# Hybrid SSD and sparse-attention layer: a new order of the weight units, and later SSD and norm steps

## What is computed

```
h = rmsnorm(x) * (1 + scale) + shift                      # scale, shift, gate from c @ w_ada
z, xbc, dt, q, kv, gates, za, mg = split(h @ w_in)
xs, B, C = split(silu(causal_conv4(xbc)))                 # 2048, 4*128, 4*128 channels
y = ssd(xs, softplus(dt), B, C) + d_skip * xs             # 2 chunks of 128, 32 heads, 4 groups
y_ssm = (rmsnorm_per_group(y * silu(z)) * g) @ w_ssm_out
kc, vc = silu(blocks(kv) @ w1) @ w2                       # 15 compressed blocks of 32 tokens
o = g0 * attend(q, kc, vc) + g1 * attend(q, ks, vs) + g2 * attend(q, kw, vw)
y_nsa = (o * silu(za)) @ w_nsa_out
out = x + gate * rmsnorm((sig(mg0) * y_ssm + sig(mg1) * y_nsa) @ w_out)
```

## Time and profile before

| | us |
|---|---|
| median of 3 runs (472.07 to 472.74) | 472.73 |
| profiled execution | 470.02 |
| its span, first to last instruction | 468.2 |
| PE busy | 438.0 |
| DVE busy | 356.2 |
| ACT busy | 259.1 |
| POOL busy | 233.9 |

### The profile page before, as it was taken

One profiled execution on the slowest core, in us unless ns is written; L12 is line 12 of the kernel. 1 busy time (PEld: TensorE's weight loads), 2 busy tenths in 40 slices (PEclk: granted clock), 3 DMA queues, 4 the chain that ended last, 5 costly groups with the idle time before them and its releaser, 6 DMA issues.

```text
span 468.2 us, 9862 instructions
## 1 busy us (share of the span) xinstructions
PE 438.0 (94%) x3636; PEld 399.7 (85%) x3636; DVE 356.2 (76%) x617; ACT 259.1 (55%) x512; POOL 233.9 (50%) x236
## 2 busy tenths in 40 slices
PE   2689989999999989999899988999999999999995
PEld 2387989999999989987898987988998989999874
DVE  0466789999999999678799986688797767547733
ACT  3235885655564653456786936566475555534441
POOL 0154662368788689755363532245355362445440
PEclk9979999999999999999999999999999999999998
DMA  7999544564424444436449550735646444456102
GB/s 280 417 415 372 182 134 136 187 191 143 158 90 146 170 137 135 136 136 241 160 183 357 162 160 0 270 98 189 256 161 243 139 136 139 165 190 228 47 0 90
DMA packets 22391, 84.04 MB, mean 179 GB/s; under 512 B 2492, under 2 KB 2882, under 8 KB 21186
## 3 DMA queue, kind: packets, MB, share of 16 engines
q1 hardware_dynamic: 22344, 83.42, 50.5%
HBM read 82.36 MB, written 1.05 MB: 178 GB/s over the span
## 4 chain that ended last, share of the span: by engine, by line
PE 69%; DVE 8%; issue 7%; ACT 5%; POOL 4%; DMA 4%; SPq 1%; DVEq 0%; POOLq 0%; ACTq 0%
PE gemm L703 14%; PE gemm L705 14%; PE gemm L704 14%; DMA w_ada_shift_scale<-in_w_ada 3%; PE y_or_o L910 2%; DVE w_lo L1191 2%; PE gemm L679 2%; ACT w_hi L932 2%; PE y_or_o L791 1%; ACT probs L1149 1%; DVE conv_acc L1238 1%; POOL w_lo L1534 1%; PE score L874 1%; PE gemm L662 1%; PE small L584 1%
## 5 line engine op out<-in xcount | busy, mean ns | idle before, releaser
L1534 POOL TENSOR_TENSOR w_lo<-w_raw,w_hi 128x256 fp32r<-128x256 f32 (+1 forms) x117 | 135.4, 1162 | 178.9 <-ACT w_hi L932 144.2
L703 PE MATMUL gemm<-h_hi,w_hi 128*128 128x256 f32 x600 | 172.3, 287 | 4.5 <-DVE conv_acc L1238 2.0
L705 PE MATMUL gemm<-h_hi,w_lo 128*128 128x256 f32 x600 | 167.2, 279 | 0.0
L704 PE MATMUL gemm<-h_lo,w_hi 128*128 128x256 f32 x600 | 167.2, 279 | 0.0
L1191 DVE TENSOR_TENSOR w_lo<-w_raw,w_hi 128x768 fp32r<-128x768 f32 (+1 forms) x117 | 130.8, 1118 | 38.7 <-ACT w_hi L932 38.2
L932 ACT CAST w_hi<-w_raw 128x1024 fp32r<-128x1024 f32 x117 | 122.3, 1045 | 49.4 <-PE gemm L705 29.3
L703 PEld LDWEIGHTS gemm<-h_hi,w_hi 128*128 128x128 f32 x600 | 113.3, 189 | 8.3 <-issue 2.8
L704 PEld LDWEIGHTS gemm<-h_lo,w_hi 128*128 128x128 f32 x600 | 113.0, 188 | 0.7 <-issue 0.2
L705 PEld LDWEIGHTS gemm<-h_hi,w_lo 128*128 128x128 f32 x600 | 113.1, 188 | 0.0
L703 PE MATMUL gemm<-ynorm_hi,w_hi 128*128 128x256 f32 x128 | 36.4, 284 | 0.0
L705 PE MATMUL gemm<-ynorm_hi,w_lo 128*128 128x256 f32 x128 | 35.6, 278 | 0.0
(11 more groups left out here) (252 smaller groups left out, 895.0 us busy)
## 6 DMA issues: line engine op xcount, KB each, us to landing
w_raw<-in_wpack SPq DMA_DIRECT2D x133, 512.0 KB, 4.4
w_ada_shift_scale<-in_w_ada SPq DMA_DIRECT2D x8, 1024.0 KB, 15.8
x_T<-in_xT SPq DMA_DIRECT2D x2, 512.0 KB, 6.2
x_residual<-in_x_tok SPq DMA_DIRECT2D x1, 1024.0 KB, 4.8
out_tok_dram<-out_tok SPq DMA_DIRECT2D x4, 256.0 KB, 2.1
ada_gate_products<-in_gate_bias SPq DMA_DIRECT2D x1, 512.0 KB, 4.5
g_post_rows<-in_g_post_rows SPq DMA_DIRECT2D x1, 512.0 KB, 5.6
consts<-in_consts SPq DMA_DIRECT2D x1, 272.0 KB, 22.1
```

Source lines behind the costliest of these rows:

```text
L703: nc.tensor.matmul(bank[:, 0:SEQ], w_hi, hi[:, k0 + k, :], start=first, stop=False)
L704: nc.tensor.matmul(bank[:, 0:SEQ], w_hi, lo[:, k0 + k, :], start=False, stop=False)
L705: last = nc.tensor.matmul(bank[:, 0:SEQ], w_lo, hi[:, k0 + k, :], start=False, stop=end)
L1534: nc.gpsimd.tensor_tensor(WL[:, n % LO_SLOTS, c:1024], RAW[:, u % RAW_SLOTS, c:1024], WH[:, n % HI_SLOTS, c:1024], ALU.subtract).then_inc( ...
```

## The change

From unit 10 on, the conv tiles c1 to c3 and x0 to x15 alternate with z0 to z15 and za0 to za4; the last of these stand alone. Units 0 to 9 and from 50 on are as before. The number of units and instructions is the same, and every unit's work is the same.

The cb steps go from units 15–17 to 18–20. The SSD groups start at b = 25 + 8g, five units later, and in the last group all from y6 on one unit later still: y6 at 54, y7 at 58, ysq3 at 59, ysum3 at 61 (before: 48, 52, 53, 55). blk0 and blk1 move by five units for the first three groups and the last stands at 43 and 44. ssq1 goes from unit 58 to 64. Norm tiles 0 to 7 stay where they are at their first step (units 51 to 61); tile 8 starts at unit 66 instead of 62, and the rest follows to unit 75. kcp goes from unit 61 to 63, and W2 is loaded after unit 63 instead of unit 60. The squares' sums get a place of their own, so POOL's clearing of k_lo no longer waits for ssq1.

```diff
--- before.py
+++ after.py
@@ -1,3 +1,5 @@
+import itertools
+
 import numpy as np
 
 import concourse.bass as bass
@@ -40,10 +42,10 @@
 def weight_units():
 
     units = [("pair", i, half) for half in range(2) for i in range(len(PAIRS))]
-    units += [("c", j, 0) for j in range(1, 4)]
-    for g in range(SSM_GROUPS):
-        units += [("x", TPG * g + j, 0) for j in range(TPG)] + [("z", TPG * g + j, 0) for j in range(TPG)]
-    units += [("za", j, 0) for j in range(5)]
+    convs = [("c", j, 0) for j in range(1, 4)] + [("x", j, 0) for j in range(TPG * SSM_GROUPS)]
+    gates = [("z", j, 0) for j in range(TPG * SSM_GROUPS)] + [("za", j, 0) for j in range(5)]
+    for conv, gate in itertools.zip_longest(convs, gates):
+        units += [conv, gate] if conv else [gate]
     for n, part in enumerate((0, 2)):
         units += [("w1k", 0, part), ("w1k", 0, part + 1), ("za", 5 + n, 0)]
     for split, part in ((("za", 7, 0), 0), (None, 2)):
@@ -100,26 +102,27 @@
     put(10, ("dtC", 0))
     put(13, ("acs", 0))
     for kind in range(3):
-        put(15 + kind, ("cb", kind))
+        put(18 + kind, ("cb", kind))
     for g in range(SSM_GROUPS):
-        b = 20 + 8 * g
+        b = 25 + 8 * g
+        last = g == SSM_GROUPS - 1
         put(b, ("xt", (g, 0)))
         put(b + 1, ("xt", (g, 1)), ("seg", 2 * g))
         put(b + 2, ("ea", 2 * g))
-        put(b + 4, ("y", 2 * g), ("seg", 2 * g + 1))
-        put(b + 5, ("ea", 2 * g + 1))
-        last = g == SSM_GROUPS - 1
-        put(b + 7 + last, ("y", 2 * g + 1))
-        put(b + 8 + last, ("ysq", g))
-        put(b + 10 + last, ("ysum", g))
+        put(b + 4 + last, ("y", 2 * g), ("seg", 2 * g + 1))
+        put(b + 5 + last, ("ea", 2 * g + 1))
+        put(b + 7 + 2 * last, ("y", 2 * g + 1))
+        put(b + 8 + 2 * last, ("ysq", g))
+        put(b + 10 + 2 * last, ("ysum", g))
     for g in range(KV_GROUPS):
-        put(18 + 8 * g, ("blk0", g))
-        put(19 + 8 * g, ("blk1", g))
+        put(min(23 + 8 * g, 43), ("blk0", g))
+        put(min(24 + 8 * g, 44), ("blk1", g))
     put(47, ("clear", 0))
     put(48, ("ssq", 0))
-    put(58, ("ssq", 1))
+    put(64, ("ssq", 1))
     tiles = TPG * SSM_GROUPS
-    norm_units = [u for u in range(50, len(UNITS)) if UNITS[u][0] not in NATIVE or UNITS[u][2] % 2]
+    norm_units = [u for u in range(50, 62) if UNITS[u][0] not in NATIVE or UNITS[u][2] % 2]
+    norm_units = norm_units[:tiles // 2] + list(range(66, len(UNITS)))
     for j in range(tiles + 2):
         for ahead, name in ((2, "ynlo"), (1, "ynhi"), (0, "yn")):
             if 0 <= j - ahead < tiles:
@@ -127,7 +130,7 @@
     at = UNITS.index
     put(at(("w1k", 0, 3)) + 2, ("hidT", 0))
     put(at(("w1v", 0, 3)) + 2, ("hidT", 1))
-    put(at(("w1v", 0, 3)) + 1, ("kcp", 0))
+    put(at(("w1v", 0, 3)) + 3, ("kcp", 0))
     put(at(("w1v", 0, 3)) + 4, ("vcp", 0))
     put(at(("vs", 1, 0)) + 2, ("vt", 0))
     put(at(("w1v", 0, 3)) + 3, ("zero", 0))
@@ -314,7 +317,7 @@
     V = place("v", [P, 2, 2, KV_GROUPS, HEAD_DIM], f32)
     over_at = cursor[0]
     kb = 1024
-    assert over_at + 50 * kb <= 229344, over_at
+    assert over_at + 52 * kb <= 229344, over_at
 
     ADA = place("w_ada_shift_scale", [P, 2, KT, 1024], f32, at=z_at)
     XT = place("x_T", [P, KT, SEQ], f32, at=over_at)
@@ -336,7 +339,7 @@
     CE = place("cb_decay_across", [P, 4, P], f32, at=over_at + 14 * kb)
     SQ = place("y_sq", [P, 4, SEQ], f32, at=over_at + 16 * kb)
     YT = place("y_tmp", [P, 2, SEQ], f32, at=over_at + 20 * kb)
-    SQS = place("y_sq_sums", [P, SSM_GROUPS, SEQ], f32, at=q_at + 28 * kb)
+    SQS = [place(f"y_sq_sums{n}", [P, 2, SEQ], f32, at=over_at + (22, 50)[n] * kb) for n in range(2)]
     RN = place("rstd_y", [P, SSM_GROUPS, SEQ], f32, at=q_at + 32 * kb)
     BLK = place("cmp_blocks", [P, 2, 16, KV_GROUPS * N_CMP], f32, at=over_at + 24 * kb)
     KVC = place("kv_cmp_T", [P, 4, SEQ], f32, at=over_at + 32 * kb)
@@ -538,7 +541,7 @@
                     else:
                         sp.wait_ge(native_mm, NATIVE_IDX[v] + 1)
                 sp.dma_start(RAW[:, u % RAW_SLOTS, :], wpack[u]).then_inc(w_in[u % RAW_SLOTS], 16)
-                if u == UNITS.index(("w1v", 0, 0)) + 4:
+                if u == UNITS.index(("w1v", 0, 0)) + 7:
                     wait_y_full(sp, ("y", 7))
                     sp.dma_start(W2[:], w2_dram).then_inc(w2_in, 16)
                 if u == UNITS.index(("kw",1,0)):
@@ -798,7 +801,7 @@
                     key = step + (0,)
                     bank = begin_small(key)
                     pe.wait_ge(ysum_done, 2 * i + 2)
-                    last = nc.tensor.matmul(bank[:, :], cst("ones"), SQS[:, 2 * i:2 * i + 2, :].rearrange("p g l -> p (g l)"),
+                    last = nc.tensor.matmul(bank[:, :], cst("ones"), SQS[i][:].rearrange("p g l -> p (g l)"),
                                             start=True, stop=True)
                     end_small(last, key)
                 elif what == "hidT":
@@ -1598,7 +1601,7 @@
 
                     pool.wait_ge(ysq_done, i + 1)
                     link(nc.gpsimd.tensor_tensor(SQ[:, 0:2, :], SQ[:, 0:2, :], SQ[:, 2:4, :], ALU.add))
-                    nc.gpsimd.tensor_tensor(SQS[:, i, :], SQ[:, 0, :], SQ[:, 1, :], ALU.add).then_inc(ysum_done, 1)
+                    nc.gpsimd.tensor_tensor(SQS[i // 2][:, i % 2, :], SQ[:, 0, :], SQ[:, 1, :], ALU.add).then_inc(ysum_done, 1)
                 elif what == "ea":
                     wait_small_out(pool, key)
                     g = i // 2
@@ -1622,7 +1625,6 @@
                     wait_zeros(pool, "p_cmp")
                     nc.gpsimd.memset(Q2[64:128].bitcast(f32), 0.0).then_inc(zeros, 1)
                     wait_zeros(pool, "q2")
-                    wait_small_full(pool, ("ssq", 1, 0))
                     nc.gpsimd.memset(KL[64:128].bitcast(f32), 0.0).then_inc(zeros, 1)
                     wait_zeros(pool, "k_lo")
                 elif what == "q2":
```

## The result

The changed kernel takes **482.45 us** (median of 4, 482.13 to 483.65) against 472.40 (median of 4): ratio 1.0217, 95% interval 1.0202 to 1.0233, 10 us slower. The profiled execution took 482.44 us, its span 480.6, 12.4 more than the span of before; the profiled execution of before lay 2.4 us under its median, so the profiles differ by 2.4 us more than the medians.

A forecast was written before the change was run, and what follows sets the result against it. PE, busy 94% of the span, was taken as the bound, with DVE a second bound in two stages. Terms 4.2 + 1.2 + 0.5 − 1.3 − 0.7 = +3.9 us gave a median of 476.6, range 471.0 to 480.5.

The forecast's parts named there:

- Can DVE start the stretch sooner?: DVE's start at unit 70's split, stretch running to head 0's first reduction: no shift, 0, bounds −1.2 and +0.8 us.
- Norm work in the stretch, 4.2: DVE, unit 70's split to head 0's first reduction: one more low part, three products, one reciprocal; +4.2 us.
- Table load, 1.2: ACT's exponential table load falls between head 0's first reduction and first exponential: +1.2 us, bounds 0 and 1.3.
- y6, +0.5: Compression: y6 follows seg6 by 5.7 us instead of 8.5, so PE waits for POOL's product; +0.5 us, at most 1.7.
- Unit 13's 1.3: PE's 1.3 us wait for a conv accumulator at unit 13 stays, with the same tile, bank and DVE steps.
- The hidden tile's 1.5: PE's 1.5 us wait for the compressed hidden tile is kept, though y7 adds DVE work before it; bound +1.7.
- y4, −1.3: PE's 1.3 us wait before y4 for POOL's product goes, since alternating conv tiles make ACT's squares and decay early.
- rival 4: The alternation does nothing, POOL's product stays as late: +5.2 us, 477.9; shares the main case's chance of 0.53.
- hid_v_T, −0.7: PE's 0.7 us wait for hid_v_T goes, as ACT has no norm copies then and ssq1 stands between; −0.7 us.
- The signs named beforehand: Profile after: no y4 or hid_v_T wait, DVE idle units 62–65, 24 us stretch, table load before first exponential, PE waiting 4 us.
- Rival 3: Compression overflows: y6 waits 1.7 us rather than 0.5, hidden tile 1.7 more; +6.8 us, 479.5; chance 0.12.
- Rival 1: Conv, POOL, hidden tile and hid_v_T waits all go and norm work finds room: −2.5 us, 470.2; chance 0.20.

The follow-up runs named there:

- vcp_first: Changed kernel with one swap: PE issues the second compression product vcp ahead of the last norm sum ssq1; 479.12 us, ratio 1.0150.
- before_light_12: Kernel before with its last four norm tiles moved to the light merge units, behind 86 and 89; 469.19 us, ratio 0.9934.
- spread_norms_vcp_first: Changed kernel with the last eight norm tiles' steps moved behind units 78 to 87 and vcp issued ahead of ssq1; 479.44 us, ratio 1.0147.
- alibi_later: Changed kernel with SP's alibi loads and their wait for vcp moved behind the load of unit 69 instead of 67; 482.18 us, ratio 1.0211.

## Why the prediction was wrong

The direction was right, the size was not: +3.9 predicted, +10 measured, outside the range. By its steps:

- **"Can DVE start the stretch sooner? ... I take 0; bounds −1.2 and +0.8."** This step failed: +3.62. I read ACT's line from unit 68's weights to unit 70's split and left the weights where they were. I had looked at what kcp and ssq1 compute, not at which of the two banks each then takes, nor at SP, whose wait for vcp stands ahead of unit 68's load. What I did read was right: ACT's row grew by 1.2, and DVE's margin of 1.1 behind it took that up. The weights came 3.5 later, and that is the miss. vcp_first takes all 3.6 away with one swap.
- **Norm work in the stretch, 4.2:** right but 0.5 short, 4.70; the counts are those predicted (7 low parts, 7 products, 2 reciprocals, 24.50 for 24.0 us), the products took 0.65 us rather than 0.62, and DVE idled 1.2 us of the stretch instead of 0.6.
- **Table load, 1.2:** right, 1.26. By the Trainium skill (ScalarE: Activation LUTs, What ACT_TABLE_LOAD costs) a drain of 1380 ns would come on top; the exponential starts 0.01 us after the load's 1.28, so the trace again disagrees.
- **y6, +0.5:** right, 0.61. Unit 13's 1.3 stayed. The hidden tile's 1.5 became 2.0.
- **y4, −1.3:** wrong, 1.38 stayed. POOL idled 4.09 us for ACT's decay, as the 4.10 of the earlier trace rows, though conv tiles now come every second unit; so it was not a row of conv tiles that held it, and what did stays open. This is rival 4's condition, and its 477.9 lacked (2) and the clock.
- **hid_v_T, −0.7:** the wait went, and the one for k_cmp took its place. Both gains would have been ahead of the stretch anyway, where what counts is when unit 68's weights and unit 66's products are there: they did not belong in the sum as they stood.
- **What no step held: the clock.** The waits cost more than their length, since PE comes out of them at 1.2 GHz: 0.9 to 1.7 us behind head 1's scores, and part of (2).

In the profiles the miss adds up. It is 3.6 for the start; 1.5 for the terms −1.3, −0.7 and +0.5, which lie ahead of the stretch and are inside that start, whatever came of them; 0.5 for the norm work, 0.1 for the load, and 2.0 for the tail. That makes 7.7, which is the 11.6 measured behind unit 13 less the 3.9 predicted.

The signs named beforehand came with one exception: DVE idled around units 62 to 65 (6.49 us ahead of 248.07), the stretch was 24.5 us, the table load stood directly ahead of the first exponential, and PE waited 4.76 us for probabilities. The wait before y4 did not go. None of them watched unit 68's weights, so they could hold while the time was 6 us off.

Rival 3 named the compression, but the waits it put there (y6 and the hidden tile) stayed small. The sign that would have spoken for it, over 3 us, did not come. Rival 1 fell with the alternation's worth. The sum of what was measured is 3.6 + 4.7 + 1.3 + 2.0 = 11.6 of the 12.4 in the profiles, and 0.8 is chance at the start. The medians differ by 10.0 only, since the profile of before lay 2.4 us under its median.

## What to carry to other kernels

When a step is moved past another, list what it shares and not only what it computes: the rotating bank, each queue that waits for it, and what is behind that wait. On an engine that will be full soon, work that is held back is lost twice, as idle time now and as length of the chain later. Hold back only what the idle time cannot take, and put it where neither its own engine nor the one that it hands over to has a critical step next; the length of a single wait on an engine that another one holds up tells little of what its removal gives: ahead of head 1's scores it was 4.65 to 4.76 us in seven kernels with medians from 477.86 to 484.30.

## What the hardware showed that was not expected

The granted clock also falls where PE does not stand. In before_light_12 PE is busy throughout. Its compressed scores, 32 products of 32 columns each, and the windows around them:

```profile
273.26 4.37 PE L855 MATMUL small<-k_cmp_hi_lo,q_hi_lo 128*128 128x32 f32 x32
```

```profile
272.00:276.00 4.00, 4.00 (x39) 4.00 (x37) 3.87 (x11) 0.37 (x1) 1.85 (x3) 1.00 0.58 196
276.00:282.00 6.00, 6.00 (x30) 6.00 (x30) 2.30 (x5) 1.91 (x8) 0.00 (x0) 0.50 0.00 0
```

The 24 products of the next unit follow each other by 0.21 us instead of 0.117, 2.2 us lost. The same fall, for a whole unit behind the same step, is in seven profiles of this case; in an eighth (spread_norms_vcp_first) it covers 15 products, and in the other nine, before and after among them, it is missing. In all seven the 32 small products themselves take 4.1 to 4.5 us instead of 3.64, so it costs some 2.9 us together. It may be part of why executions of one kernel differ by up to 6 us (alibi_later, where the slower ones have the lower mean clock); only one execution of each has a profile, so that is not shown. In before_light_12 it is more than the whole tail of +1.94. What decides whether it comes was not tried.
